# The distance bias of a causal attention: 128 stored copies read at a pitch one value shorter, in place of three flipping products

## The reference, cut to what matters

```python
buckets = t5_bucket(jnp.arange(S))               # S = 256
bias_dist = rel_bias[buckets].T                  # (4 heads, 256 distances)

def block(args):                                 # blocks of 128 queries
    qa, qc, start = args
    qpos = start + jnp.arange(128)
    dist = qpos[:, None] - kpos[None, :]
    bias = bias_dist[:, jnp.clip(dist, 0, S - 1)]
    def probs(q, k):
        s = einsum('bqhd,bkhd->bhqk', q, k) * scale + bias
        s = where(dist >= 0, s, -inf)
        return softmax(s)
    a = probs(qa, k1) - lam * probs(qc, k2)
    return einsum('bhqk,bkhd->bqhd', a, v)
```

## Time and profile before

| | us |
|---|---|
| median of 3 runs | 1111.45 |
| the runs | 1111.63, 1109.93, 1111.45 |
| span of the profiled execution | 1110.0 |
| PE busy | 1085.4 |
| DVE busy | 726.5 |
| ACT busy | 522.2 |
| POOL busy | 64.6 |

### The profile page before, as it was taken

How to read it: one execution, slowest core, us unless ns; L and a number is a source line. 1 busy time by engine, 2 the same in 40 slices (tenths; PEclk the granted TensorE clock), 3 DMA queues, 4 the chain that set the end, 5 groups by cost and what they waited for, 6 DMA issues and landing times.

```text
span 1110.0 us, 14044 instructions
## 1 busy us (share of the span) xinstructions
PE 1085.4 (98%) x5862; PEld 930.2 (84%) x5862; DVE 726.5 (65%) x769; ACT 522.2 (47%) x591; POOL 64.6 (6%) x116
## 2 busy tenths in 40 slices
PE   6999999999999999999999999999999998999998
PEld 4989898898888888998888888887888876888887
DVE  4756565467777677666646877768667477564654
ACT  5555555354444445434445454444564464453441
POOL 2200000000000000000001000001201010000000
PEclk9999999999999999999999999999999999999999
DMA  9834454456786755554545768674334363655531
GB/s 357 342 129 171 153 208 152 170 180 229 263 335 212 298 188 209 177 191 160 214 138 208 279 259 328 221 298 157 124 131 168 147 247 114 227 190 190 190 114 39
DMA packets 32351, 224.95 MB, mean 203 GB/s; under 512 B 3748, under 2 KB 4064, under 8 KB 7584
## 3 DMA queue, kind: packets, MB, share of 16 engines
q1 hardware_dynamic: 26640, 188.03, 46.3%
q0 software_dynamic: 5120, 34.85, 8.8%
q10 hardware_dynamic: 528, 1.16, 0.3%
HBM read 222.95 MB, written 1.08 MB: 202 GB/s over the span
## 4 chain that ended last, share of the span: by engine, by line
PE 93%; DVE 4%; ACT 1%; issue 1%; POOL 1%; DMA 0%; DVEq 0%; ACTq 0%; POOLq 0%
PE ps L525 47%; PE ps L509 19%; PE ps L484 10%; PE ps L511 10%; PE ps L585 1%; DVE lo L1602 1%; PE ps L765 1%; PE ps L786 1%; DMA h<-in_x 0%; PE ps L943 0%; PE ps L989 0%; DVE lo L1594 0%; DVE h L1653 0%; ACT hi L1109 0%; PE ps L922 0%
## 5 line engine op out<-in xcount | busy, mean ns | idle before, releaser
L1602 DVE TENSOR_TENSOR lo<-raw,hi 128x2048 fp32r<-128x2048 f32 x163 | 372.8, 2289 | 182.5 <-ACT hi L1109 182.3
L1109 ACT ACTIVATE hi<-raw 128x2048 fp32r<-128x2048 f32 x163 | 311.8, 1915 | 266.8 <-PE ps L525 152.5
L509 PE MATMUL ps<-xt,hi 128*128 128x512 f32 x896 | 317.5, 399 | 0.0
L511 PE MATMUL ps<-xt,lo 128*128 128x256 f32 x896 | 251.3, 280 | 0.0
L525 PE MATMUL ps<-hi,yt_hi 128*128 128x512 f32 x544 | 213.0, 392 | 2.4 <-DVE yt_lo L1905 1.4
L525 PE MATMUL ps<-lo,yt_hi 128*128 128x512 f32 x544 | 211.8, 389 | 0.0
L525 PE MATMUL ps<-hi,yt_lo 128*128 128x512 f32 x544 | 211.8, 389 | 0.0
L509 PEld LDWEIGHTS ps<-xt,hi 128*128 128x128 f32 x896 | 168.3, 188 | 41.3
L511 PEld LDWEIGHTS ps<-xt,lo 128*128 128x128 f32 x896 | 169.2, 189 | 0.6
L525 PE MATMUL ps<-hi,xt 128*128 128x512 f32 x384 | 131.4, 407 | 4.8 <-issue 3.1
L525 PEld LDWEIGHTS ps<-hi,yt_hi 128*128 128x128 f32 x544 | 102.1, 188 | 24.6 <-issue 3.5
(11 more groups left out here) (257 smaller groups left out, 1054.4 us busy)
## 6 DMA issues: line engine op xcount, KB each, us to landing
raw<-in_weights SPq DMA_DIRECT2D x176, 1024.0 KB, 4.9
work<-in_w_ada POOLq DMA_DIRECT2D x16, 1536.0 KB, 7.6
work<-in_gains POOLq DMA_DIRECT2D x6, 512.0 KB, 4.1
work<-mod_rows POOLq DMA_DIRECT2D x6, 512.0 KB, 6.1
h<-in_x SPq DMA_DIRECT2D x2, 512.0 KB, 6.2
work<-in_gains ACTq DMA_DIRECT2D x2, 512.0 KB, 7.2
work<-in_mem POOLq DMA_DIRECT2D x2, 512.0 KB, 9.2
work<-in_pool SPq DMA_DIRECT2D x1, 1024.0 KB, 14.8
```

What stands on the lines that cost most here:

```text
L509: pe.matmul(o, hi[:, slot, k, js], flat(x[2][:, c]), start=(c == 0), stop=False, skip_group_check=True)
L511: mm = pe.matmul(o[:, 0:S], lo[:, slot, k, js], x[0][:, c, :], start=False, stop=(c == KC - 1), skip_group_check=True)
L1109: act.activation(hi[:, p % RING], raw[:, p % RING], ACT.Copy).then_inc(hi_ready, 1)
L1602: dve.tensor_tensor(lo[:, p % RING], raw[:, p % RING], hi[:, p % RING].bitcast(F32), ALU.subtract)\
```

## The change

The store writes each of the four rows 128 times, so that the HBM tensor is (4, 128, 384) in place of (4, 384): copy p of a head begins 384 values after copy p - 1. The two loads take partition p from copy p with a pitch of 383 values, one less than a copy is long, which moves the table by one value per partition in the direction that is needed. The load of `flip_m`, the three products of `bias_turned` and the three copies on DVE are removed. POOL's first mask now waits for the two loads instead of for DVE's copies.

```diff
-    flip_m, bucket_m, rel, bias_row = w(10240, P), w(10368, 384), w(10752, 4), w(10756, 384)
+    bucket_m, rel, bias_row = w(10368, 384), w(10752, 4), w(10756, 384)
...
-    rows_dram = nc.dram_tensor("bias_rows", (4, 384), F32, kind="Internal").ap()
+    rows_dram = nc.dram_tensor("bias_rows", (4, P, 384), F32, kind="Internal").ap()
...
-            pe.wait_ge(loaded["rel"], 48)
+            pe.wait_ge(loaded["rel"], 32)
...
-        def bias_turned():
-
-            pe.wait_ge(loaded["flipped"], 32)
-            for n, src in ((0, flip1[:, 0:2, :]), (1, flip1[:, 2:4, :]), (2, flip0)):
-                o = claim(4 + n, ("bias", n))
-                filled_by(pe.matmul(o, flip_m, flat(src), start=True, stop=True), ("bias", n))
...
-        unit_w(UNIT["l0_k"], XT, (0, 1), hooks={(1, 0): bias_turned})
+        unit_w(UNIT["l0_k"], XT, (0, 1))
...
-        act.dma_start(flip_m, d["flip"]).then_inc(loaded["rel"], 16)
...
-        for n, dst in ((0, bias1[:, 0:2, :]), (1, bias1[:, 2:4, :]), (2, bias0)):
-            label = ("bias", n)
-            dve.wait_ge(*fill(label))
-            dve.tensor_copy(dst, cut(bank(label), dst.shape[1])).then_inc(*free(label))
...
-        gp.dma_start(rows_dram, bias_row[0:4, :]).then_inc(bias_stored, 16)
+        gp.dma_start(rows_dram, bias_row[0:4, :].rearrange("p (a b) -> p a b", a=1).to_broadcast((4, P, 384)))\
+            .then_inc(bias_stored, 16)
         gp.dma_start(cols[:, :], d["cols"]).then_inc(loaded["consts"], 16)
         gp.dma_start(lam_in, d["lam"].to_broadcast((P, 4, 64))).then_inc(loaded["lam"], 16)
         for t in range(T):
             gp.dma_start(mem_rows[:, t, :], d["mem"][t * P:(t + 1) * P, :]).then_inc(loaded["mem"], 16)
         gp.wait_ge(bias_stored, 16)
-        for dst, offset, n in ((flip1, 0, S), (flip0, P, P)):
-            src = bass.AP(tensor=rows_dram.tensor, offset=offset, ap=[[1, P], [384, 4], [1, n]])
-            gp.dma_start(dst, src).then_inc(loaded["flipped"], 16)
+        for dst, offset, n in ((bias1, P - 1, S), (bias0, S - 1, P)):
+            src = bass.AP(tensor=rows_dram.tensor, offset=offset, ap=[[383, P], [384 * P, 4], [1, n]])
+            gp.dma_start(dst, src).then_inc(loaded["bias"], 16)
...
-        gp.wait_ge(*read(("bias", 1)))
+        gp.wait_ge(loaded["bias"], 32)
...
-        gp.wait_ge(*read(("bias", 2)))
```

More of the change, by code:

```diff
@@ L129, in constants @@
     c["ident"] = np.eye(P, dtype=f)
-    c["flip"] = np.eye(P, dtype=f)[::-1].copy()
     dist = np.maximum(S - 1 - np.arange(384), 0)
@@ L243, in program @@
     bias1, bias0 = w(3072, 4, S), w(4096, 4, P)
-    flip1, flip0 = bias1, bias0
     kv_k, kv_v = w(5120, KC, S), w(7168, T, D)
@@ L307, in program @@
     ada_landed, ada_used = sem("ada_landed"), sem("ada_used")
-    loads = (["x0", "x1", "ident", "mem", "consts", "rel", "lam", "pool", "flipped", "c", "ff", "const2", "decay",
+    loads = (["x0", "x1", "ident", "mem", "consts", "rel", "lam", "pool", "bias", "c", "ff", "const2", "decay",
               "scale_m", "shift_m", "gate_m", "scale_f", "shift_f", "gate_f"]
```

## The result

The changed kernel takes 1130.09 us (median of 5 runs, 1129.31 to 1130.54), the one before 1111.45 us in the same comparison (1109.93 to 1112.67): a ratio of 1.0167, 95% interval 1.0157 to 1.0178. It is 18.6 us slower; 16.8 were forecast.

The account below looks back on a forecast made before the run. PE, busy for 98% of the span, was taken to bound the kernel. The terms -2.6 + 17.7 + 1.7 = +16.8 us on 1111.45 gave 1128 us, range 1108 to 1140.

Parts of the forecast that it names:

- The flipping products: Three products alone on PE's chain between two halves; removing them was to save 2.6 us.
- The copies and the load of flip_m: DVE's three copies (1.88 us) beside PE's work and a load in ACT's queue; removing them was to gain 0.
- The store: POOL's store of the rows, 6 KB grown to 786 KB from four partitions; expected to take 30.2 us more.
- slow end: The 786 KB store at the rate of one DMA engine, 26 GB/s: 30.2 us; the case the forecast took.
- (c): Rival: each of the store's four rows gets its own engine share, 7.6 to 15.1 us; 1108.9 to 1113.2 us; chance 0.10.
- What stands behind it: `lam_in`, queued behind the store, lands at 52.7 us against a latest time of 35.0; PE stands before `l0_k`: +17.7 us.
- The clock: PE's granted clock drops once after the long pause, as at 776 to 782 us: +1.7 us, bounds 0 and 3.4.
- slower cases: The outcomes in which the change slows the kernel, chance 0.68, with their own range of 1120 to 1140 us.
- What was late next: `mem`, landing behind `lam_in`, and POOL's wait for the store; covered by 12.8 us and the pause: 0.
- (a): Rival: the store waits for the weights' 12.0 us on its engine; `lam_in` lands at 64.7 us; 1140 us; chance 0.18.
- (b): Rival: the store runs at full rate, 1.9 us, nothing waits, only the flipping products go; 1108.9 us; chance 0.19.
- (d): Rival: the store is harmless and PE waits elsewhere for the 2.6 us, so no effect; 1111 us; chance 0.03.

Follow-up runs that it names:

- experiment 2: Changed kernel with the old 6 KB store and loads at the old pitch and offsets, so only the flipping products go (wrong bias): 1109.02 us, ratio 0.9976.
- 3: Changed kernel with `rel` held 32 times, the same 786 KB stored from 128 partitions, four copies from each: 1109.09 us, ratio 0.9972.
- 4: Changed kernel with each head on four partitions, the store reading partitions 0, 4, 8 and 12: 1113.04 us, ratio 1.0014.
- 5: Changed kernel with each head on four neighbouring partitions, the store reading all 16, 32 copies from each: 1109.22 us, ratio 0.9976.
- 9: Changed kernel with 64 copies in place of 128 (393 KB) and loads at a pitch of 190 values (wrong bias): 1113.07 us, ratio 1.0012.
- Experiment 7: Changed kernel with the store issued behind `cols`, `lam_in` and `mem`, and POOL's wait and two loads behind the roots of `mem`: 1116.12 us, ratio 1.0038.
- 8: Changed kernel with the wide store issued from ACT's queue instead of POOL's, its source at the place of `bias1`: 1112.63 us, ratio 1.0011.
- experiment 1: Kernel before with only the wide store, loads reading the first copy at the old pitch, flipping products kept: 1135.86 us, ratio 1.0220.
- 11: Changed kernel storing from 128 partitions, with the two loads reading each head's first copy at a pitch of one value (wrong bias): 1108.51 us, ratio 0.9972.

## Why the prediction was right

**The flipping products, -2.6 us.** Right: 2.6 us in experiment 2. In the chain of after the two halves of `l0_k` join.

**The copies and the load of flip_m, 0.** DVE has 1.7 us less to do, of 1.9 expected; PE's first transposes began 0.1 us earlier. Experiment 2 holds all of it within its 2.6 us.

**The store.** It took 37.7 us from its issue, 35.3 were forecast (5.1 + 30.2). Taking off the 5.1 us, 786 KB in 32.6 us are 24.1 GB/s, against the 26 of the slow end, and from 40 to 50 us POOL's queue moved 24. That the narrow source makes the store slow is now shown (3, 4, 5), where before the run it was an argument. The reason behind the number was not right: the slow end was the rate of one engine, and the share of 0.26 is that of four. That the rate of one engine and the rate at which four neighbouring partitions can be read lie so close was luck. The Trainium skill's figure of 27.6 GB/s for partitions 0 to 3 ("SBUF — State Buffer", "Door 1: The DMA port swizzle") lies near the 24.1 that were measured beside other traffic, and its reason, neighbouring partitions that share a port, agrees with experiment 4. Its other rule, that the slowest dimension of both sides sets the number of engines ("DMA: Bandwidth & Descriptors", "Why a DMA increments its semaphore by 16 and not by 1"), agrees too: the share of 0.26 is four of sixteen. In the prediction I made these two into separate cases, (c) against the forecast. They hold together: four engines, and behind them one way out of the four partitions. Rival (c) by itself is what experiment 4 built, and it came out at 1113.0 us, at the upper end of the 1108.9 to 1113.2 that (c) gave.

**What stands behind it, +17.7 us.** 19.9 were measured. `lam_in` landed at 54.3 instead of 52.7 us, and the distance from there to half 4 was 5.2 us, 4.8 forecast. The latest time of 35.0 us held in three kernels (4, 9 and the changed one), to 0.6 us.

**The clock, +1.7 us.** Under-sized. Against the earlier trace rows, the granted clock of after:

```profile
55.00:60.00 5.00, 0.43 (x2) 0.43 (x3) 3.28 (x10) 4.90 (x6) 0.00 (x0) 0.50 0.55 213
60.00:65.00 5.00, 5.00 (x25) 5.00 (x25) 5.00 (x4) 5.00 (x8) 0.11 (x1) 0.50 0.93 322
65.00:70.00 5.00, 5.00 (x42) 5.00 (x40) 3.89 (x4) 2.67 (x5) 4.42 (x4) 0.94 1.04 372
```

The lower level (1.2 GHz) was still granted after PE had resumed at 59.57 us, until some way into the stretch from 65. The two halves of `l0_k` took 14.43 us where two halves are 2 x 5.76 = 11.5 us: 2.9 us lost. After the short pauses of 4 and 9 (3.1 and 2.9 us) the two halves took 13.08 and 13.27 us, 1.6 and 1.8 us lost, as in the earlier trace rows; a short pause was not a measure of the price after a long one.

**The sum.** 19.9 + 2.9 - 2.6 = 20.2, and the spans differ by 18.5. The remaining 1.7 us are the dip of the clock at 776 to 782 us in the profile of before, which that of after does not have at the same place of the program:

```profile
797.00:800.00 3.00, 2.64 (x12) 2.19 (x13) 2.81 (x5) 2.44 (x4) 2.08 (x4) 1.00 0.00 0
800.00:803.00 3.00, 3.00 (x19) 2.49 (x17) 3.00 (x3) 2.15 (x4) 0.00 (x0) 1.00 0.00 0
```

The change did not take it away: of the two kernels without a pause before `l0_k`, 2 has this dip in its profile and 3 does not. My forecast of 16.8 was 1.8 us low for two terms that were 2.2 and 1.2 us low, against which this one stood. That it stood against them is luck; without it the forecast would have been 3.4 us low. The 1130.09 us lie inside the 1120 to 1140 of the slower cases; the whole range, 1108 to 1140, also took in the faster rival and would have borne out little.

**What was late next, 0.** True in the changed kernel, and true only because the pause covered it. I had looked at `mem`, not at the weights: the prediction weighed them only as something that slows the store (a), not as something that the store slows. Experiment 7 puts that at 5.2 us of waiting for PE when `lam_in` is not the first to be late. A fix that had moved the small loads alone, by the prediction's own reasoning, would have been forecast at 1109 and taken 1116.

**The rivals.** (b) fell with the row of the store in the issues of after (37.7 us), and (d) with the time. (a), the store waiting for all the weights' work, needed 12 us more than the forecast and gave 1140; the store took 2.4 us more.

## What to carry to other kernels

Before a small store is made large, look at how many partitions it leaves from: 786 KB cost 32.6 us from four neighbouring partitions, 15.7 from four that lie apart, 6.0 from sixteen and 2.8 from 128, beyond the small store's time. Then look at what stands behind it in its queue and on its engines, and give each its latest time: here the wait that decided was for 128 KB that have nothing to do with the bias. When the first late thing is mended, forecast again, because a long pause hides the second.

## What the runs showed of the hardware that I had not expected

A slow store in one queue can make transfers of another queue late: a half of the weights took 26.3 us in place of 4.9 (experiment 7), and from 45 to 50 us of that time three quarters of the engines were free. From ACT's queue the same store did this far less (8). In the changed kernel, in the store's last stretch, the DMA share was 0.26 and the rate 44 GB/s, so a low share can go with a blocked stream.

Reading one copy of each head by 128 partitions, each one value on, with the heads 196,608 bytes apart, holds the engines at a full share for 184 to 193 GB/s (experiment 1, below) and 282 to 292 (11). The same pitch with the heads 1,536 bytes apart, in the kernel before, ran in a stretch of 396 GB/s and landed after 10.3 us. What in the addresses does it was not tried.

```profile
55.00:60.00 5.00, 0.96 (x4) 0.96 (x5) 3.37 (x4) 5.00 (x4) 0.00 (x0) 0.50 1.02 184
60.00:65.00 5.00, 5.00 (x27) 5.00 (x26) 5.00 (x4) 5.00 (x10) 0.56 (x1) 0.53 1.01 193
```
